# Prompt attention of a two-layer decoder: both score maps turned in one block, 64-row score tiles, 1024-column score operations, longer leads between engines

## What is computed

```python
qs = q.reshape(bsz, tq, h, 2, DIFF_DH)            # DIFF_DH = 64, two maps
ks = k.reshape(bsz, tk, h, 2, DIFF_DH)
s = jnp.einsum('bqhmd,bkhmd->bhmqk', qs, ks).astype(F32) * (DIFF_DH ** -0.5)
s = s + bias[None, :, None]                       # by distance; constant beyond 128 positions
s = jnp.where(rel >= 0, s, jnp.finfo(F32).min)    # causal
p = jax.nn.softmax(s, axis=-1)
a = p[:, :, 0] - lam * p[:, :, 1]                 # difference of the two maps
return jnp.einsum('bhqk,bkhd->bqhd', a, v.astype(F32))
```

## Time and profile before

| | us |
|---|---|
| median of 3 runs (lowest to highest) | 3955.66 (3954.72 to 3956.73) |
| profiled execution, its own time | 3956.0 |
| its span, first to last instruction | 3954.2 |
| prompt attention, first combine to last combine | 844.3 |
| a head within it | 106.2 to 114.1, the last 86.5 |

### The profile page before, as it was taken

How to read it: one execution, slowest core, us unless ns; L and a number is a source line. 1 busy time by engine, 2 the same in 40 slices (tenths; PEclk the granted TensorE clock), 3 DMA queues, 4 the chain that set the end, 5 groups by cost and what they waited for, 6 DMA issues and landing times. The chain is left out here.

```text
span 3954.2 us, 55321 instructions
## 1 busy us (share of the span) xinstructions
PE 3629.8 (92%) x19279; PEld 2987.5 (76%) x19279; DVE 2020.6 (51%) x4394; ACT 1323.2 (33%) x2186; POOL 319.5 (8%) x258
## 2 busy tenths in 40 slices
PE   3999997996999999999999688888898799969999
PEld 3988985774888888888888577777777767558887
DVE  1112111555732642743733588889888222156785
ACT  1112111331221322322322366666666211123332
POOL 0002002111100300200200000000000000022220
PEclk9999997998999999999999899999999899989999
DMA  4323332335334434445443622222210545254541
GB/s 111 98 90 120 102 96 80 112 112 196 115 128 133 165 123 159 160 129 166 147 136 122 134 66 66 55 53 55 66 34 12 205 176 206 106 185 165 170 159 71
DMA packets 364126, 473.00 MB, mean 120 GB/s; under 512 B 157877, under 2 KB 219094, under 8 KB 363878
## 3 DMA queue, kind: packets, MB, share of 16 engines
q1 hardware_dynamic: 363878, 469.77, 37.8%
HBM read 365.20 MB, written 104.47 MB: 119 GB/s over the span
## 5 line engine op out<-in xcount | busy, mean ns | idle before, releaser
L438 PE MATMUL mid_ps_m<-mid_w_hi,mid_x_hi 128*128 128x512 f32 x1632 | 641.0, 393 | 0.5 <-DVE mid_x_lo L594 0.5
L439 PE MATMUL mid_ps_m<-mid_w_lo,mid_x_hi 128*128 128x512 f32 x1632 | 635.8, 390 | 0.0
L440 PE MATMUL mid_ps_m<-mid_w_hi,mid_x_lo 128*128 128x512 f32 x1632 | 635.7, 390 | 0.0
L606 DVE TENSOR_TENSOR mid_w_lo<-mid_stage,mid_w_hi 128x1024 fp32r<-128x1024 f32 x192 | 239.1, 1246 | 234.8 <-ACT mid_w_hi L524 233.4
L438 PE MATMUL in_ps_m<-in_w_hi,in_x_hi 128*128 128x512 f32 (+2 forms) x952 | 344.9, 362 | 12.6 <-DVE in_x_lo L594 12.6
L440 PEld LDWEIGHTS mid_ps_m<-mid_w_hi,mid_x_lo 128*128 128x128 f32 x1632 | 306.7, 188 | 64.3
L438 PEld LDWEIGHTS mid_ps_m<-mid_w_hi,mid_x_hi 128*128 128x128 f32 x1632 | 306.8, 188 | 63.5 <-DVE mid_x_lo L594 1.7
L439 PEld LDWEIGHTS mid_ps_m<-mid_w_lo,mid_x_hi 128*128 128x128 f32 x1632 | 306.9, 188 | 61.4
L440 PE MATMUL in_ps_m<-in_w_hi,in_x_lo 128*128 128x512 f32 (+2 forms) x952 | 343.4, 361 | 0.0
L439 PE MATMUL in_ps_m<-in_w_lo,in_x_hi 128*128 128x512 f32 (+2 forms) x952 | 343.4, 361 | 0.0
L1502 PE MATMUL att_ps_o<-att_v,att_a_t 128*128 128x128 f32 x2176 | 291.8, 282 | 47.0 <-ACT att_a_t L1563 46.1
(11 more groups left out here) (278 smaller groups left out, 5622.0 us busy)
## 6 DMA issues: line engine op xcount, KB each, us to landing
mid_stage<-in_diff_w_in SPq DMA_DIRECT2D x128, 512.0 KB, 3.7
smp_k_pg<-in_cache_k SPq DMA_DIRECT2D x64, 512.0 KB, 5.1
smp_v_pg<-in_cache_v SPq DMA_DIRECT2D x64, 512.0 KB
in_stage<-in_gla_w_in SPq DMA_DIRECT2D x32, 512.0 KB, 4.0
mid_stage<-in_gla_w_out SPq DMA_DIRECT2D x32, 512.0 KB, 5.5
mid_stage<-in_ple_w_gate SPq DMA_DIRECT2D x32, 512.0 KB, 3.5
att_k_nat<-out_k SPq DMA_DIRECT2D x128, 128.0 KB, 2.6
att_q_nat<-diff_q SPq DMA_DIRECT2D x128, 128.0 KB, 2.8
```

Of the source, the lines that this page charges most:

```text
L438: nc.tensor.matmul(dst, x_hi[u][:, k, :], w_hi[r][:, i, 0:W], start=(k == 0), stop=False)
L439: nc.tensor.matmul(dst, x_hi[u][:, k, :], w_lo[r][:, i, 0:W], start=False, stop=False)
L440: mm = nc.tensor.matmul(dst, x_lo[u][:, k, :], w_hi[r][:, i, 0:W], start=False, stop=(k == KD - 1))
L606: nc.vector.tensor_tensor(lo, stage[n % STAGES][:, :, 0:W], hi.bitcast(F32), ALU.subtract).then_inc(s["w_lo_done"], 1)
```

## The change

- q and k are loaded once, and one transpose turns both maps: map 0 comes to lie in rows 0 to 63 and map 1 in rows 64 to 127. There are 8 prep blocks per head where there were 16. ACT only copies a block out (`raw`); POOL makes hi and lo.
- A score is three matmuls of 64 rows, hi x hi, hi x lo and lo x hi, and the two maps' matmuls stand alternately in PE's list, each in its half of the rows.
- Score pieces are up to 1024 keys of both maps, each map in a two-bank PSUM slot, of which there are three (`SLOTS`). One DVE operation with the bias table (widened to 2048 columns, filled by POOL) takes a piece of one map.
- One PSUM bank (`ps_a`) serves all transposes, where there were three.
- `inv` and `weight` move to POOL (`row_weight`); the scaled output moves from ACT to DVE; `neg` is one operation.
- The leads: PE makes scores 4 tiles ahead (`LEAD`), DVE takes 3 ahead (`TAKE`), ACT's exponentials run 2 ahead (`EXP`), with four score buffers in SBUF. In PE's list the score pieces are spread between the value steps of tile n, behind the first of them.
- The loop over heads is written out in full.

```diff
-    RING = 4
-    beside = [1] * T
+    WIDE = 2 * BANK
+    LEAD, TAKE, EXP = 4, 3, 2
+    S_BUFS, SLOTS, OUTS = 4, 3, 4
...
+        ps_s = [ps(f"ps_s{i}", WIDE) for i in range(SLOTS)]
+        ps_a = ps("ps_a")
         ps_o = ps("ps_o")
...
-                            dst = ps_s[n % RING][:, 0:hi_ - lo_]
-                            lhs = q_hl[u][m][:, i * P:(i + 1) * P]
-                            nc.tensor.matmul(dst, lhs, k_hi[u][m][:, lo_:hi_], start=True, stop=False)
-                            nc.tensor.matmul(dst, lhs, k_lo[u][m][:, lo_:hi_], start=False,
-                                             stop=True).then_inc(s["piece_ready"], 1)
+                        if x + 2 > SLOTS:
+                            pe.wait_ge(s["taken"], after(x + 2 - SLOTS))
+                        for a0 in range(first, last, BANK):
+                            a1 = min(a0 + BANK, last)
+                            for step, (left, right) in enumerate(((hi, hi), (hi, lo), (lo, hi))):
+                                for m in range(2):
+                                    rows = slice(m * D_DH, (m + 1) * D_DH)
+                                    mm = nc.tensor.matmul(ps_s[(x + m) % SLOTS][:, a0 - first:a1 - first],
+                                                          left[u][1][rows, i * P:(i + 1) * P],
+                                                          right[u][0][rows, a0:a1], start=(step == 0),
+                                                          stop=(step == 2))
+                            if a1 == last:
+                                mm.then_inc(s["ready"], 1)
                             yield
...
+                def values(n):
+                    for g in range(turns(n) + 1):
+                        if g < turns(n):
+                            turn(n, g)
+                            yield
+                        if g >= 1:
+                            meet(n, g - 1)
+                            yield
+
+                for n in range(FIRST, N):
+                    for key in preps_at(n):
+                        prep(*key)
+                    ahead = sum(-(-(b - a_) // BANK) for a_, b in parts(n + LEAD)) if 0 <= n + LEAD < N else 0
+                    mixed = scores(n + LEAD) if ahead else iter(())
+                    steps = 2 * turns(n) if n >= 0 else 0
+                    done = 0
+                    for m, _ in enumerate(values(n) if n >= 0 else ()):
+                        while done * steps < ahead * (m + 1):
+                            next(mixed, None)
+                            done += 1
+                    for _ in mixed:
+                        pass
...
+                for n in range(FIRST, N):
+                    ahead = 0 <= n + EXP < N
+                    if ahead:
+                        exps(n + EXP, 0)
+                    for key in preps_at(n):
+                        evict(*key)
+                    middle = (turns(n) + 1) // 2 if n >= 0 else 0
+                    copies(n, 0, middle)
+                    if ahead:
+                        exps(n + EXP, 1)
+                    copies(n, middle, turns(n) if n >= 0 else 0)
...
+                    nc.gpsimd.tensor_copy(hi[u][which][:, cols], raw[m % 2][:, :]).then_inc(s["hi_done"], 1)
+                    pool.wait_ge(s["hi_done"], after(m + 1))
+                    nc.gpsimd.tensor_tensor(lo[u][which][:, cols], raw[m % 2][:, :],
+                                            hi[u][which][:, cols].bitcast(F32), ALU.subtract
+                                            ).then_inc(s["lo_done"], 1)
...
+                            nc.vector.tensor_tensor_reduce(
+                                out=s_sb[n % S_BUFS][:, m, first:last], in0=ps_s[(x + m) % SLOTS][:, 0:last - first],
+                                in1=bias[u][:, SEQ - keys(n) + first:SEQ - keys(n) + last], scale=1.0,
+                                scalar=-3.0e38, op0=ALU.add, op1=ALU.max,
+                                accum_out=mx[n % 2][:, m, c:c + 1]).then_inc(s["taken"], 1)
...
-                    for i in range(T):
-                        if not (last and i + 1 >= T):
-                            take(*ahead(H, u, i, 1))
-                        combine(H, u, i)
-                        if not last:
-                            for n, (is_q, m, g) in enumerate(slots(i)[0]):
-                                low(H + 1, 1 - u, slots(i)[1] + n, is_q, m, g)
+                for n in range(-TAKE, N + 1):
+                    if n + TAKE < N:
+                        take(n + TAKE)
+                    if 0 <= n < N:
+                        combine(n)
+                    if 1 <= n:
+                        output(n - 1)
```

More of the change, by code:

```diff
@@ L1354, in attention @@
[L1354 to L1360, removed]
+        mx = [sb(f"mx{i}", [P, 2, 2]) for i in range(2)]
+        neg = [sb(f"neg{i}", [P, 2]) for i in range(S_BUFS)]
+        total = [sb(f"total{i}", [P, 2]) for i in range(S_BUFS)]
@@ L1506, in values @@
[L1506 to L1512 removed]
+                        pe.wait_ge(s["a_done"], after(n + 1))
+                    wait_bank_free(turn_use[(n, g)])
+                    for b in range(4 * g, min(4 * g + 4, n % T + 1)):
+                        mm = nc.tensor.transpose(ps_a[:, (b % 4) * P:(b % 4 + 1) * P], a[n % 2][:, b * P:(b + 1) * P],
+                                                 core.ident[:, :])
@@ L1533, in _ @@
-                for n, (is_q, m, g) in enumerate(preps):
-                    prep(0, n, is_q, m, g, turn_banks)
-                for i in range(2):
-                    for _ in scores(0, 0, i):
+                for n in range(FIRST, N):
[10 more added lines that the diff above has]
+                    for _ in mixed:
@@ L1589, in _, with evict @@
-                for n, (is_q, m, g) in enumerate(preps):
-                    high(0, 0, n, is_q, m, g, turn_banks)
-                for m in range(2):
-                    exps(0, 0, 0, m)
-                over_heads(act, head)
+                def evict(h, j):
+                    m = prep_no[(h, j)]
+                    act.wait_ge(s["turned"], after(prep_use[(h, j)] + 1))
+                    if m >= 2:
+                        act.wait_ge(s["lo_done"], after(m - 1))
+                    nc.scalar.activation(raw[m % 2][:, :], ps_a[:, :], ACT.Copy,
+                                         scale=D_DH ** -0.5 if j % 2 else 1.0).then_inc(s["raw_done"], 1)
@@ new lines, in exps @@
+                def exps(n, m):
+                    act.wait_ge(s["max_done"], after(n + 1))
+                    if n >= S_BUFS and m == 0:
+                        act.wait_ge(s["weight_done"], after(n - S_BUFS + 1))
+                        act.wait_ge(s["o_copied"], after(n - S_BUFS + 1))
+                    nc.scalar.activation(s_sb[n % S_BUFS][:, m, 0:keys(n)], s_sb[n % S_BUFS][:, m, 0:keys(n)], ACT.Exp,
+                                         bias=neg[n % S_BUFS][:, m:m + 1],
+                                         accum_out=total[n % S_BUFS][:, m:m + 1]).then_inc(s["exp_done"], 1)
```

431 lines of the change are left out of this document (196 added, 235 removed).

## The result

The changed kernel takes **4252.96 us** (median of 4 runs, 4247.84 to 4257.48), the kernel before 3955.19 beside it: a ratio of **1.0752**, 95% interval 1.0739 to 1.0765. The forecast was 4210 us, with a range of 4020 to 4380.

A forecast was written before the change was run, and what follows sets the result against it. An unhidden PE-DVE round trip per tile was taken to bound it: 129 us a head plus 10 for the clock, stage +261, lead-in -7, on 3956.0 giving 4210 us; range 4020 to 4380.

The forecast's parts named there:

- The chain: PE scores, DVE's last take and combine, PE's transposes: an unshortened round trip per tile, 129.0 us a head against 106.2.
- Its length: Round trips per four-tile group of a head: 24.0, 29.2, 45.6 and 30.2, together 129.0 us a head before clock losses.
- The switch: PE changing between 64-row score pieces and 128-row matmuls: 0.2 us each, 60 on the path, 12 us a head.
- The maps side by side: Both maps' 64-row score matmuls run concurrently on PE, so a 512-key piece costs 0.69 us, not 1.38.
- the case of 4369: Rival: the two maps' score matmuls run one after the other, 19.9 us a head more, 4369 us; chance 0.15.
- The floor of 0.67 us for a short piece: A short score piece on PE takes no less than six weight loads at 0.112 us, 0.67 us.
- The clock: Half clock for 3.4 us behind PE's pauses, in about nine of 16 tiles: 10 us a head, bounds 0 and 15.
- The sum: Stage from first combine to last: 8 heads of 139 us less 6.8, 1105 us against 844.3, +261.
- What was costed at nothing: Splits and weights moved to POOL, some 22 us a head for splits, weights with two tiles of slack: no cost.
- DVE's takes: One DVE operation with the bias table on 1024 keys takes 1.15 us, with 82 ns fixed for each operation.
- The signs: Heads at 129 to 139 us, DVE busy near 68, PE under 100, both waiting on each other once per tile.
- No chain, PE bounds: Rival: the four-tile lead hides the round trip, PE's work of 94 us a head sets about 3850 us; chance 0.11.

The follow-up runs named there:

- filled_pauses: Changed kernel plus 3 to 11 extra 512-column matmuls on PE at the end of each of a head's first twelve tiles; 4122.98 us.
- combine_first: Changed kernel with the combine of tile n + 1 moved ahead of the take of tile n + 4 in DVE's list; 3933.62 us.
- the grouping: Score pieces of one part (up to 1024 keys) together in PE's list: 4090.19 us on the changed kernel, 3850.91 with the combine also one tile earlier.
- narrow: Changed kernel with score parts of 512 keys in six slots instead of 1024 in three; 4104.47 us.

## Why the prediction was right, point by point

- *The chain* was right: one moved call in DVE's list takes 319 us away, and the same order put into the kernel before adds 172.
- *Its length* was right in the sum, in part by luck. At full clock filled_pauses measures 128.1 us a head against 129.0 worked out. By groups of four tiles, from combine to combine in head 3 of that run: 27.1, 30.3, 44.2 and 26.5, where 24.0, 29.2, 45.6 and 30.2 stood. The first and the last group are off by 3 and 4 us in opposite directions, and this cancels: tile 0's transposes also stand behind the last value matmuls of tile 15 (its combine ends at 2604.1, they start at 2608.6), and the estimates for the last group, of which ACT was thought the bound, were too long.
- *The switch*, 0.2 us taken: 0.17 each by tile 10's rows, 0.15 to 0.22 by PE's busy time over 256 switches. The Trainium skill ("TensorEngine Tiling (Array Packing)", section "Tiling Modes") says that a change of mode drains TensorE; this case's runs agree in that each change has a cost, by these numbers.
- *The maps side by side*, 0.69 us a piece: right for a full piece, and the case of 4369 falls. The floor of 0.67 us for a short piece was wrong: at full clock pairs of 128 columns follow each other at 0.11 us (2669.31 to 2669.42 in filled_pauses), so three of them make some 0.33. The rule of the Trainium skill ("TensorE: Matmul & The Clock Gate", section "Part 3: Packing small matmuls — row/col tiling") on row groups that run concurrently agrees with the pairs at one spacing of 0.23 us.
- *The clock* was the term that was mis-sized, in the prediction's words "I take 10 (bounds 0 and 15)": 130 us come back when the pauses are filled, 16.3 a head, which is above the upper bound. I had counted nine stretches of 3.4 us like that of the earlier trace rows, 31 us a head; the 390 us are 49 a head. The count of pauses was near (82 of 1.55 us and more, ten a head), but the time at the lower level behind each was longer, by the estimate above 4.9 us. The price of it was as taken: a third of a us for each us at the lower level (10 for 31, 16.3 for 49).
- The sum: the stage was put at 1105 and is 1147.5. The clock makes +54 (134 against 80), the loop -12 (1013.2 against 1025), half of it in the last head, which takes 116.2 at full clock where 122.2 stood (129.0 less 6.8). The time from the first combine backwards was right to 0.3 us (-7.3 against -7).
- *What was costed at nothing* held: POOL's weights and splits end no wait of DVE or PE in the changed kernel's stage, and its weights end 4 us of DVE's in combine_first. DVE's saving of 178 us in the stage doesn't show in the time while the loop is closed.
- *DVE's takes*: the starts of the two takes of 1024 keys lie 1.15 us apart (2743.37 to 2744.52), as worked out. The 82 ns of an operation come from such a spacing (0.35 us at 256 keys); by the durations of the earlier trace rows that stand beside it they would be 152, and one take of 1024 keys does last 1.23.
- *The signs*: the heads, at 140 to 147 us, lie above the 129 to 139, and PE's 106 to 113 us a head above "under 100", both with more work at the lower clock than was taken. DVE's 69 us and the two waits came as named. The chain of what ended last doesn't reach back to this stage, so that sign can't be read.
- *No chain, PE bounds* was the rival of the other sign, at 3850. It is not what the change does. With the moved call PE does come near to setting the time, at 3934, or 3851 with the grouping too; that 3851 meets the rival's number is chance, as the rival counted all 80 switches a head.

## What to carry to other kernels

A lead of several tiles doesn't hide a round trip if each of two in-order lists puts its wait for the other ahead of the work that the other waits for; follow one tile round both lists, from result to result, before counting busy time. Cutting the work of an engine that waits in such a loop gains only what lies on the loop itself (here 178 us less of DVE's work went with a slower kernel), and longer operations can lengthen the loop, since the last one must be complete before the other side may go on (narrow: 148 us less with more work). Where a loop leaves TensorE pauses, price the lower clock behind each of them too: here it was 130 of the 298 us lost.

## What the runs showed of the hardware

Extra matmuls whose result nobody reads made the kernel 130 us faster, since the granted clock stayed at 1.00 instead of 0.83 in the stage. Of PE's 97 waits for the combine the 15 of up to 1.42 us were followed by a clock of 1.00, and 80 of the 82 of 1.55 us and more by the lower level. Two pauses of 3.3 us at the same place of two heads had different sequels, 0.50 and 1.00, and what decides between them stays open: no run was made for it. Pairs of 64-row matmuls on the two halves share one spacing, 0.23 us at 512 columns and 0.11 at 128, and the switch between them and 128-row matmuls costs 0.15 to 0.22 us.
